# Row tiles turned by a product with identity times root, and first products made tile by tile, in an encoder step

## The chip, the cores and the metric

The kernel runs on one core of one Trainium2 chip. The metric is device time in microseconds, the median of repeated runs. The kernel before the change takes 1940.13 us (three runs, 1940.03 to 1941.39). One execution of it was profiled: 1939.99 us, with a span of 1938.3 us from its first profiled instruction to its last.

## The reference, cut to what matters

One layer of a streaming encoder is computed for 1024 new frames of a prompt and 32 frames of a running stream, 1056 tokens of width 2048 in all:

```
h = rms_norm(x, norm_pre)            # x * rsqrt(mean(x*x) + 1e-6) * gain
p = h @ w_in                         # 2048 x 6656, split into three groups of heads
o = concat(stick-breaking attention, sliding window, chunk band), each times silu(gate)
y = x + rms_norm(o @ w_out, norm_post)
```

All inputs are float32. The change touches `rms_norm(x, norm_pre)`, the transposition of its result, and the first of the 128-column tiles of `h @ w_in`.

## The kernel before, in words

TensorE contracts over partitions, so `h` has to lie with its 2048 features on partitions: `act_hi` and `act_lo`, each 128 x 16 x 1056 (feature within a block, block, token). `act_hi` is the value rounded to the reduced float32 type (fp32r), `act_lo` is what the rounding left. A weight piece is split in the same way into `w_hi` and `w_lo`, and a product is three fp32r matmuls: `w_hi` with `act_hi`, `w_hi` with `act_lo`, `w_lo` with `act_hi` (lines 1194, 1195, 1196 in `product`). The weights are the operand that stays in the array and are loaded before each matmul (LDWEIGHTS); the activations are the operand that moves through it.

The tokens come in nine row tiles, eight of 128 tokens and one of 32. For each row tile `t`:

- SyncE loads it into one of four buffers `x_t` (line 1031); tile `t + 4` waits until tile `t` has been transposed.
- ScalarE squares it with a sum per row (`x_squares`, line 1490). GpSimd makes the variance of that (line 2128), ScalarE a first guess of the reciprocal root by a logarithm and an exponential (`x_guess`, lines 1496 and 1498), GpSimd refines it with four tiny instructions (lines 2130 to 2136).
- VectorE multiplies the row tile by the root and by the norm weights in one instruction over 2048 columns (`x_scale`, line 1738).
- TensorE transposes the 16 blocks of 128 columns in four groups of four, each group into one PSUM bank (`x_tile`, line 1184). The block is the operand that stays, the identity the one that moves.
- ScalarE copies each bank to `act_hi` (`x_high`, line 1503) and VectorE subtracts that from the bank into `act_lo` (`x_low`, line 1745).

The tokens also form three groups of 352 for the projection, one PSUM bank each. The first weight tile has four pieces (`q` = 0 to 3, four blocks of features each). Its pieces are rounded by ScalarE (`high`, line 1508) and split by VectorE (`low`, line 1753) after row tile 2. `first_project(g, quarters)` runs `product(g, q)`, 12 matmuls of 352 moving columns: group 0 after row tiles 3, 4 and 5, group 1 after row tiles 6, 7 and 8, group 2 after all. Each of these calls follows `x_tile(t)` in TensorE's order, which is the order of the program text. VectorE's order is `x_scale(0)`, then for each `t`: `x_scale(t + 1)`, `x_low(t)`, and after `t` = 2 the four `low`.

After that a plan that is fixed in the program interleaves the other 51 weight tiles with attention (`pe_plan`), and last comes the output projection. SyncE issues the loads of weight pieces in its own planned order; a piece of the second weight tile waits until the last use of the piece before it (`piece_used`, raised by group 2).

Of the kernel before, what the change touches and what calls it, by code (L numbers as in the profile page):

```python
# [10 lines left out]
P = 128  # L11
# [529 lines left out]
def build(nc, x_prompt, x_sample, cache_a_k, cache_a_v, cache_b_k, cache_b_v, cache_c_k, cache_c_v,  # L541
# [3 lines left out]
    with ctx:  # L545
# [12 lines left out]
        def sem(name):  # L558
            return ctx.enter_context(nc.semaphore(name))
# [43 lines left out]
        x_t = [arena[:, o:o + D] for o in (1152, 1152 + D, 1152 + 2 * D, 1152 + 4 * D + D // 2)]  # L603
        pre_gain = arena[:, 1152 + 3 * D:1152 + 4 * D]
        squares_x = arena[:, 1152 + 4 * D:1152 + 4 * D + D // 2].bitcast(BF16)

# [93 lines left out]
        def bank(b, n=512, r=P, c=0):  # L700
            return ps[0:r, 512 * b + c:512 * b + c + n]
# [49 lines left out]
        x_in = [sem(f"x_in{i}") for i in range(4)]  # L751
        gain_in = sem("gain_in")
        x_sq, x_var, x_ln, x_std, x_rstd, x_norm = (sem(n) for n in ("x_sq", "x_var", "x_ln", "x_std", "x_rstd", "x_norm"))
# [420 lines left out]
        def _(pe):  # L1174
            mm = nc.tensor.matmul

            def x_tile(t):
                rows = rows_of(t)
                for g in range(4):
                    pe.wait_ge(x_norm, t + 1)  # L1180
                    if t:
                        pe.wait_ge(x_lo, 4 * t + g - 3)
                    for c in range(4):
                        last = nc.tensor.transpose(bank(X + g, rows, P, rows * c),
                                                   x_t[t % 4][0:rows, P * (4 * g + c):P * (4 * g + c) + P],
                                                   ident[0:rows, 0:rows])
                    last.then_inc(xt_done, 1)
# [22 lines left out]

            def first_project(g, *quarters):
                pe.wait_ge(x_lo, 4 * (3 * g + 3))
                for q in quarters:
                    pe.wait_ge(lo_made, q + 1)
                    last = product(g, q)
                    if q == 3:
                        last.then_inc(proj_done, 1)
                    elif g == GROUPS - 1:
                        last.then_inc(piece_used, 1)

            def set_ready(key):
# [202 lines left out]
            for t in range(TT + 1):  # L1424
                x_tile(t)

                if t >= 3:
                    first_project(t // 3 - 1, *((0,), (1, 2), (3,))[t % 3])
            first_project(GROUPS - 1, 0, 1, 2, 3)

# [51 lines left out]
        def _(act):  # L1482
# [9 lines left out]
            def x_guess(t):  # L1492
                rows = rows_of(t)
                r = std_x[0:rows, t % 3:t % 3 + 1]
                act.wait_ge(x_var, t + 1)
                fn(r, var[0:rows, t:t + 1], ACT.Ln).then_inc(x_ln, 1)
                act.wait_ge(x_ln, t + 1)
                fn(r, r, ACT.Exp, scale=-0.5).then_inc(x_std, 1)
# [7 lines left out]
            def high(T, q):  # L1506
                act.wait_ge(raw_in[q], RAW[T])
                fn(w_hi[:, q, :], w_raw[:, q, :], ACT.Copy).then_inc(hi_made, 1)  # L1508
# [4 lines left out]
            for t in range(TT + 1):  # L1513

                if t < TT - 1:
                    x_squares(t + 2)
                x_high(t, 0)
                x_high(t, 1)
                if t < TT - 1:
                    x_guess(t + 2)  # L1520
                x_high(t, 2)
                x_high(t, 3)
                if t == 2:
                    for q in range(4):
                        high(0, q)

# [196 lines left out]
        def _(dve):  # L1723
            v = nc.vector

            v.memset(qbd[:, :], 0.0).then_inc(zeroed, 1)

            dve.wait_ge(rel_in, 16)
# [4 lines left out]

            def x_scale(t):
                rows = rows_of(t)
                r = std_x[0:rows, t % 3:t % 3 + 1]
                dve.wait_ge(x_rstd, 4 * t + 4)
                v.scalar_tensor_tensor(x_t[t % 4][0:rows, :], x_t[t % 4][0:rows, :], r, pre_gain[0:rows, :],  # L1738
                                       ALU.mult, ALU.mult).then_inc(x_norm, 1)

# [13 lines left out]

            x_scale(0)
            for t in range(TT + 1):
                if t < TT:
                    x_scale(t + 1)
                x_low(t)
                if t == 2:  # L1760
                    for q in range(4):
                        low(q)

# [340 lines left out]
        def _(pool):  # L2104
# [7 lines left out]
            for m in (ident, ident_b):  # L2112
# [8 lines left out]
                             pattern=[[1, DEC]], channel_multiplier=-1).then_inc(consts, 1)  # L2121

            for t in range(TT + 1):

# [3 lines left out]
                gp.tensor_scalar(var_, ssq[0:rows, t:t + 1], 1.0 / D, EPS, ALU.mult, ALU.add).then_inc(x_var, 1)  # L2128
                pool.wait_ge(x_std, t + 1)
                gp.tensor_tensor(nt, r, r, ALU.mult).then_inc(x_rstd, 1)  # L2130
                pool.wait_ge(x_rstd, 4 * t + 1)
# [3 lines left out]
                pool.wait_ge(x_rstd, 4 * t + 3)  # L2135
                gp.tensor_tensor(r, r, nt, ALU.mult).then_inc(x_rstd, 1)

            gp.memset(mask_c[:, :], 0.0).then_inc(consts, 1)
# [103 lines left out]
```

## Time and profile before

| | |
|---|---|
| median of three runs | 1940.13 us |
| profiled execution | 1939.99 us |
| its span | 1938.3 us |
| TensorE busy in the span | 1907.4 us (98%) |
| VectorE busy | 1221.8 us (63%) |
| ScalarE busy | 667.4 us (34%) |
| GpSimd busy | 51.9 us (3%) |

A profile page names engines PE (TensorE matmul), PEld (TensorE weight load, which overlaps PE), DVE (VectorE), ACT (ScalarE), POOL (GpSimd) and SP (SyncE). Times are microseconds from the start of the span, unless marked ns. Matmuls are pipelined: the duration of one holds its way through the array, and the distance from the start of one to the start of the next is what it costs in a stream. Some matmul records are missing from a trace, so counts of long stretches run a few per cent low.

### The profile page before, as it was taken

The numbers are of one execution on the slowest core, as the hardware profiler recorded it, in microseconds if no ns is written. First come the engines' busy times: TensorE is split into PE (matmuls) and PEld (weight loads), VectorE is DVE, ScalarE is ACT, GpSimd is POOL, SyncE is SP. The second block draws the span as 40 slices with busy tenths as digits, with TensorE's granted clock in tenths as the row PEclk, the third lists the DMA queues.
The fourth block names the chain that finished last, engine by engine and source line by source line (L and its number), as shares of the span: only waits on it lengthen the run. The fifth ranks groups of instructions, "written<-read, shape, count | busy, mean of one in ns | idle before, by whom it ended". The sixth has DMA issues, their size and how long they took to land.

```text
span 1938.3 us, 31051 instructions
## 1 busy us (share of the span) xinstructions
PE 1907.4 (98%) x12604; PEld 1751.8 (90%) x12604; DVE 1221.8 (63%) x2176; ACT 667.4 (34%) x1257; POOL 51.9 (3%) x119
## 2 busy tenths in 40 slices
PE   5999999999999999999999999999999999999997
PEld 5999999999999999999999999999999988888886
DVE  7358677786877778554544454355525666766878
ACT  7124333343423334221222222233213354344453
POOL 3000000000000000000000000000000000000131
PEclk9999999999999999999999999999999999999999
DMA  6446777676777766666657657465446557555396
GB/s 245 117 115 140 156 154 166 144 147 153 151 156 155 170 139 144 157 136 134 154 117 154 147 129 143 104 145 123 107 97 145 131 195 284 192 175 187 122 257 226
DMA packets 880406, 301.05 MB, mean 155 GB/s; under 512 B 618504, under 2 KB 845592, under 8 KB 878968
## 3 DMA queue, kind: packets, MB, share of 16 engines
q1 hardware_dynamic: 877192, 290.35, 61.6%
q0 software_dynamic: 3072, 8.73, 2.2%
q8 instruction: 99, 1.62, 0.3%
q14 instruction: 43, 0.35, 0.1%
HBM read 210.45 MB, written 96.20 MB: 158 GB/s over the span
## 4 chain that ended last, share of the span: by engine, by line
PE 94%; DVE 4%; DMA 1%; issue 1%; ACT 0%; POOL 0%; DVEq 0%; SPq 0%; ACTq 0%; POOLq 0%
PE ps L1194 23%; PE ps L1195 22%; PE ps L1196 22%; PE ps L1405 4%; PE ps L1407 4%; PE ps L1406 4%; PE ps L1297 3%; PE ps L1376 3%; PE ps L1258 3%; PE ps L1347 3%; DVE arena L1738 1%; DVE act_lo L1745 1%; PE ps L1402 1%; PE ps L1401 1%; DMA arena<-in_x_prompt_dram 0%
## 5 line engine op out<-in xcount | busy, mean ns | idle before, releaser
L1194 PE MATMUL ps<-act_hi,w_hi 128*128 128x352 f32 x2688 | 877.8, 327 | 0.0
L1195 PE MATMUL ps<-act_lo,w_hi 128*128 128x352 f32 x2688 | 862.7, 321 | 0.0
L1196 PE MATMUL ps<-act_hi,w_lo 128*128 128x352 f32 x2688 | 862.6, 321 | 0.0
L1194 PEld LDWEIGHTS ps<-act_hi,w_hi 128*128 128x128 f32 x2688 | 504.6, 188 | 16.9 <-issue 14.0
L1195 PEld LDWEIGHTS ps<-act_lo,w_hi 128*128 128x128 f32 x2688 | 505.5, 188 | 0.0
L1196 PEld LDWEIGHTS ps<-act_hi,w_lo 128*128 128x128 f32 x2688 | 504.3, 188 | 0.0
L1508 ACT ACTIVATE w_hi<-w_raw 128x512 fp32r<-128x512 f32 x224 | 139.2, 623 | 344.7 <-DMA w_raw<-in_w_in_dram 344.6
L1753 DVE TENSOR_TENSOR w_lo<-w_raw,w_hi 128x512 fp32r<-128x512 f32 x224 | 150.5, 673 | 51.9 <-ACT w_hi L1508 51.7
L1575 ACT ACTIVATE arena<-arena,small 128x257 f32<-128x257 f32 (+6 forms) x180 | 101.2, 565 | 208.2 <-DVE small L1886 208.2
L2074 DVE STREAM_TRANSPOSE arena<-arena 128x1024 f32<-128x1024 f32 (+4 forms) x100 | 132.6, 1326 | 49.4 <-ACT arena L1696 48.6
L1696 ACT ACTIVATE arena<-arena 128x1024 f32<-128x1024 f32 (+1 forms) x60 | 61.1, 1018 | 251.8 <-DVE arena L1860 251.8
L1405 PE MATMUL ps<-w_hi,l_hi 128*128 128x512 f32 x280 | 109.3, 390 | 0.6 <-DVE w_lo L1944 0.3
L1407 PE MATMUL ps<-w_hi,l_lo 128*128 128x512 f32 x280 | 109.0, 389 | 0.0
L1406 PE MATMUL ps<-w_lo,l_hi 128*128 128x512 f32 x280 | 108.9, 389 | 0.0
L1886 DVE CUSTOM_DVE_ANT_0 arena<-ps,arena 128x640 f32<-128x640 f32 (+5 forms) x72 | 44.0, 660 | 85.7 <-PE ps L1297 85.7
L1836 DVE TENSOR_TENSOR arena<-ps,arena 128x1024 f32<-128x1024 f32 (+1 forms) x60 | 70.2, 1171 | 30.9 <-ACT arena L1692 30.9
L1777 DVE COPY arena<-ps 128x352 f32<-128x352 f32 x84 | 43.1, 515 | 64.9 <-PE ps L1196 63.3
L1848 DVE TENSOR_TENSOR_SCAN arena<-arena 128x512 f32<-128x512 f32 (+4 forms) x102 | 79.5, 833 | 0.8
L1692 ACT ACTIVATE arena<-arena 128x1024 f32<-128x1024 f32 (+1 forms) x60 | 61.1, 1019 | 52.2 <-DVE arena L2084 52.2
L1587 ACT ACTIVATE w_hi<-w_raw 128x512 fp32r<-128x512 f32 x70 | 44.0, 628 | 101.2 <-DVE w_raw L1923 79.0
L1688 ACT ACTIVATE arena<-ps 128x1024 f32<-128x1024 f32 (+1 forms) x60 | 58.6, 976 | 55.0 <-PE ps L1275 47.1
L1786 DVE TENSOR_SCALAR arena<-ps 128x352 f32<-128x352 f32 x48 | 25.1, 523 | 76.9 <-PE ps L1196 76.7
(183 smaller groups left out, 2097.3 us busy)
## 6 DMA issues: line engine op xcount, KB each, us to landing
w_raw<-in_w_in_dram SPq DMA_DIRECT2D x176, 256.0 KB, 3.3
weight_scratch<-arena SPq DMA_DIRECT2D x216, 128.0 KB, 3.5
arena<-weight_scratch SPq DMA_DIRECT2D x54, 512.0 KB, 4.6
b_out<-in_w_out_dram SPq DMA_DIRECT2D x72, 256.0 KB, 3.3
w_raw<-in_w_out_dram SPq DMA_DIRECT2D x70, 256.0 KB, 2.6
w_raw<-in_w_in_dram SPq DMA_DIRECT2D x96, 128.0 KB, 3.1
weight_scratch<-arena SPq DMA_DIRECT2D x80, 132.0 KB, 4.0
arena<-weight_scratch SPq DMA_DIRECT2D x40, 256.0 KB, 3.4
```

Of the source, the lines that this page charges most:

```text
L1194: mm(bank(g, GN), wh, ah, start=(k == 0), stop=False)
L1195: mm(bank(g, GN), wh, al, start=False, stop=False)
L1196: last = mm(bank(g, GN), wl, ah, start=False, stop=(k == KT - 1))
L1405: mm(out, th, wh, start=first, stop=False)
L1406: mm(out, th, wl, start=False, stop=False)
L1407: last = mm(out, tl, wh, start=False, stop=end)
L1508: fn(w_hi[:, q, :], w_raw[:, q, :], ACT.Copy).then_inc(hi_made, 1)
L1575: fn(s, s, ACT.Exp, bias=neg_max[0:rows_of(m), t:t + 1], scale=-1.0, accum_out=row_sum[0:rows_of(m), t:t + 1]).then_inc(p_exp, 1)
L1753: v.tensor_tensor(w_lo[:, slot, :], w_raw[:, slot, :], w_hi[:, slot, :].bitcast(F32), ALU.subtract).then_inc(lo_made, 1)
L1836: v.tensor_tensor(both, z, both, ALU.max).then_inc(sp_ready, 1)
L1848: v.tensor_tensor_scan(along, along, along, 0.0 if newest else carry[:, 2 * m - 8 + h:2 * m - 7 + h], ALU.add, ALU.max).then_inc(sum_ready, 1)
L2074: v.transpose(s, s).then_inc(wt_blocks, 1)
```

## The change

VectorE no longer multiplies by the root. It multiplies each row tile by the norm weights alone (`x_gain`, a tensor_tensor over 2048 columns), which no longer waits for the root: only for the row tile and for its squares (tiles 1 and 2 write to other places and don't wait for their squares). GpSimd makes a diagonal matrix for each tile, identity times root (`scale_d`), and TensorE turns each block by a plain float32 matmul with that matrix as the moving operand, where it had a transpose with the identity. GpSimd also rounds the four first weight pieces, which ScalarE did. The first guess of the root reads the sums of squares directly. The first weight tile's products are no longer made per group of 352 tokens but in column ranges a..b of groups 0 and 1, as the row tiles arrive; group 2 stays whole.

```diff
             def x_tile(t):
                 rows = rows_of(t)
                 for g in range(4):
                     pe.wait_ge(x_norm, t + 1)
+                    pe.wait_ge(diag_made, t + 1)
                     if t:
                         pe.wait_ge(x_lo, 4 * t + g - 3)
                     for c in range(4):
-                        last = nc.tensor.transpose(bank(X + g, rows, P, rows * c),
-                                                   x_t[t % 4][0:rows, P * (4 * g + c):P * (4 * g + c) + P],
-                                                   ident[0:rows, 0:rows])
+                        last = mm(bank(X + g, rows, P, rows * c), x_gained(t, rows)[:, 4 * g + c, :],
+                                  scale_d[t % 3][0:rows, 0:rows], start=True, stop=True)
...
+            def first_product(g, q, a, b):
+                for kk in range(4):
+                    k = 4 * q + kk
+                    wh, wl = w_hi[:, q, P * kk:P * kk + P], w_lo[:, q, P * kk:P * kk + P]
+                    ah, al = act_hi[:, k, GN * g + a:GN * g + b], act_lo[:, k, GN * g + a:GN * g + b]
+                    out = bank(g, b - a, P, a)
+                    mm(out, wh, ah, start=(k == 0 and a == 0), stop=False, skip_group_check=True)
+                    mm(out, wh, al, start=False, stop=False, skip_group_check=True)
+                    last = mm(out, wl, ah, start=False, stop=(k == KT - 1), skip_group_check=True)
+                return last
...
+            EARLY = {1: [(0, 0, P, 0, 1)], 2: [(0, 0, P, 2, 3), (0, P, 2 * P, 0, 1, 2, 3)], 3: [(0, 2 * P, GN, 0, 1, 2, 3)],
+                     4: [(1, 0, 4 * P - GN, 0, 1)], 5: [(1, 0, 4 * P - GN, 2, 3)],
+                     6: [(1, 4 * P - GN, GN, 0, 1)], 7: [(1, 4 * P - GN, GN, 2, 3)]}
...
-                if t >= 3:
-                    first_project(t // 3 - 1, *((0,), (1, 2), (3,))[t % 3])
-            first_project(GROUPS - 1, 0, 1, 2, 3)
+                for part in EARLY.get(t, ()):
+                    first_project(*part)
+            first_project(GROUPS - 1, 0, GN, 0, 1, 2, 3)
...
             def x_guess(t):
...
-                act.wait_ge(x_var, t + 1)
-                fn(r, var[0:rows, t:t + 1], ACT.Ln).then_inc(x_ln, 1)
+                act.wait_ge(x_sq, t + 1)
+                act.wait_ge(eps_made, 1)
+                fn(r, ssq[0:rows, t:t + 1], ACT.Ln, bias=eps_col[0:rows, :], scale=1.0 / D).then_inc(x_ln, 1)
...
+                for g in range(4):
+                    x_high(t, g)
                 if t < TT - 1:
                     x_squares(t + 2)
-                x_high(t, 0)
-                x_high(t, 1)
-                if t < TT - 1:
                     x_guess(t + 2)
-                x_high(t, 2)
-                x_high(t, 3)
-                if t == 2:
-                    for q in range(4):
-                        high(0, q)
...
-            def x_scale(t):
+            def x_gain(t):
                 rows = rows_of(t)
-                r = std_x[0:rows, t % 3:t % 3 + 1]
-                dve.wait_ge(x_rstd, 4 * t + 4)
-                v.scalar_tensor_tensor(x_t[t % 4][0:rows, :], x_t[t % 4][0:rows, :], r, pre_gain[0:rows, :],
-                                       ALU.mult, ALU.mult).then_inc(x_norm, 1)
+                dve.wait_ge(x_in[t % 4], 16 * (t // 4 + 1))
+                if t not in (1, 2):
+                    dve.wait_ge(x_sq, t + 1)
+                v.tensor_tensor(x_gained(t, rows), x_t[t % 4].rearrange("p (k c) -> p k c", c=P)[0:rows],
+                                pre_gain.rearrange("p (k c) -> p k c", c=P)[0:rows], ALU.mult).then_inc(x_norm, 1)
...
+                if t == 1:
+                    low(0)
+                    low(1)
                 x_low(t)
-                if t == 2:
-                    for q in range(4):
-                        low(q)
+                if t == 1:
+                    low(2)
+                    low(3)
...
+            def first_high(q):
+                pool.wait_ge(raw_in[q], RAW[0])
+                gp.tensor_copy(w_hi[:, q, :], w_raw[:, q, :]).then_inc(hi_made, 1)
...
+                pool.wait_ge(x_rstd, 4 * t + 4)
+                if t >= 3:
+                    pool.wait_ge(xt_done, 4 * (t - 3) + 4)
+                gp.tensor_scalar(scale_d[t % 3][0:rows, 0:rows], ident[0:rows, 0:rows], r, None, ALU.mult).then_inc(diag_made, 1)
+                if t in (1, 2):
+                    first_high(2 * t - 2)
+                    first_high(2 * t - 1)
```

`first_project(g, a, b, quarters)` waits for the row tiles that hold the tokens up to `b` of group `g` and runs `first_product(g, q, a, b)` for each quarter.

## Rows read from the trace of the kernel before

**Rows 1.** The page: shares of the span, and the chain that ended last.

```profile
PE 1907.4 (98%) x12604; PEld 1751.8 (90%) x12604; DVE 1221.8 (63%) x2176; ACT 667.4 (34%) x1257; POOL 51.9 (3%) x119
...
PE 94%; DVE 4%; DMA 1%; issue 1%; ACT 0%; POOL 0%; DVEq 0%; SPq 0%; ACTq 0%; POOLq 0%
```

**Rows 2.** Busy time by stretch: start:end, length, engines, granted clock, DMA.

```profile
12.15:50.00 37.85, 30.54 (x186) 27.31 (x187) 35.40 (x40) 34.06 (x67) 16.31 (x43) 0.95 0.60 205
57.30:65.00 7.70, 7.70 (x51) 7.70 (x50) 1.15 (x3) 1.26 (x2) 0.00 (x0) 1.00 0.30 84
65.00:1700.00 1635.00, 1635.00 (x11321) 1523.05 (x11321) 1000.29 (x1830) 515.46 (x952) 0.00 (x0) 1.00 0.65 147
```

**Rows 3.** Chain that ended last, in order of time: start, length, what.

```profile
14.60 2.35 DVE arena L1738
16.95 2.39 DVE act_lo L1745 x4
...
48.03 2.42 PE ps L1184 x16
```

**Rows 4.** Timeline of TensorE's matmuls: start, length, what, count.

```profile
12.15 3.65 PE L1184 MATMUL ps<-ident,arena 128*128 128x128 f32 x16 [12.15 <-DVE arena L1738]
17.70 3.31 PE L1184 MATMUL ps<-ident,arena 128*128 128x128 f32 x16 [1.90 <-DVE act_lo L1745]
...
54.21 1.19 PE L1184 MATMUL ps<-ident,arena 32*128 32x32 f32 x16
55.32 0.43 PE L1194 MATMUL ps<-act_hi,w_hi 128*128 128x352 f32 x1
...
55.91 0.32 PE L1194 MATMUL ps<-act_hi,w_hi 128*128 128x352 f32 x1
...
57.34 0.32 PE L1194 MATMUL ps<-act_hi,w_hi 128*128 128x352 f32 x1
...
223.66 2.00 PE L1258 MATMUL ps<-arena 64*128 64x512 f32 x12
225.59 0.51 PE L1275 MATMUL ps<-mask_b,ident_b 128*128 128x128 bf16 x6
```

**Rows 5.** Groups of matmuls by line and shape: count, busy, mean ns.

```profile
L1258 PE MATMUL ps<-arena 64*128 64x512 f32 x144 | 37.4, 624 | 0.0
```

**Rows 6.** Line 1258 alone in two short stretches: how many matmuls had begun.

```profile
223.60:223.65 0.05, 0.00 (x0) 0.00 (x0) 1.00 1.12 338
223.65:223.70 0.05, 0.04 (x2) 0.04 (x2) 1.00 1.10 328
```

**Rows 7.** Timeline of TensorE's weight loads: start, length, what, count.

```profile
54.20 1.08 PEld L1184 LDWEIGHTS ps<-ident,arena 32*128 32x128 f32 x16 [0.21 <-issue]
55.32 0.19 PEld L1194 LDWEIGHTS ps<-act_hi,w_hi 128*128 128x128 f32 x1
55.43 0.19 PEld L1195 LDWEIGHTS ps<-act_lo,w_hi 128*128 128x128 f32 x1
55.59 0.19 PEld L1196 LDWEIGHTS ps<-act_hi,w_lo 128*128 128x128 f32 x1
```

**Rows 8.** Timeline of ScalarE, VectorE and GpSimd.

```profile
7.51 0.19 ACT L1490 ACTIVATION_READ_ACCUMULATOR arena<-arena 128x1 f32 x1
...
8.24 0.20 ACT L1498 ACTIVATE small<-small 128x1 f32<-128x1 f32 x1
...
10.72 1.91 ACT L1490 ACTIVATE arena<-arena 128x2048 bf16<-128x2048 f32 x1 [2.27 <-DMA arena<-in_x_prompt_dram]
...
9.65 2.35 DVE L1738 SCALAR_TENSOR_TENSOR arena<-arena,small 128x2048 f32<-128x2048 f32 x1 [2.40 <-POOL small L2136]
...
54.98 1.05 DVE L1745 TENSOR_TENSOR act_lo<-ps,act_hi 128x128 fp32r<-128x128 f32 x4 [0.66 <-ACT act_hi L1503]
...
8.52 0.19 POOL L2130 TENSOR_TENSOR small<-small 128x1 f32<-128x1 f32 x1 [0.55 <-ACT small L1498]
8.79 0.19 POOL L2132 TENSOR_TENSOR small<-small 128x1 f32<-128x1 f32 x1
...
15.45 1.55 POOL L2128 TENSOR_SCALAR small<-small 128x1 f32<-128x1 f32 x1 [0.89 <-ACT arena L1490]
```

**Rows 9.** VectorE's split of the first weight pieces, and GpSimd's nearest 128x128 operation.

```profile
28.57 2.49 DVE L1753 TENSOR_TENSOR w_lo<-w_raw,w_hi 128x512 fp32r<-128x512 f32 x4
...
2.87 0.29 POOL L2113 TENSOR_SCALAR_AFFINE_SELECT ident<-ident 128x128 f32<-128x128 f32 x1 [0.24 <-POOL mask_s L2110]
```

More of the change, by code:

```diff
@@ L604, in build, with x_gained @@
         pre_gain = arena[:, 1152 + 3 * D:1152 + 4 * D]
+        eps_col = small[:, 149:150]
+        x_early = place("x_early", [P, KT, TOK], F32, 0, 0)
+        scale_d = [arena[:, 12416 + P * i:12416 + P * i + P] for i in range(3)]
+        def x_gained(t, rows):
+            if t == 1:
+                return raw[:, :, SEQ - P:SEQ]
+            if t == 2:
+                return x_early[:, :, SEQ - P:SEQ]
+            return x_t[t % 4].rearrange("p (k c) -> p k c", c=P)[0:rows]
         squares_x = arena[:, 1152 + 4 * D:1152 + 4 * D + D // 2].bitcast(BF16)
@@ L751, in build @@
         x_in = [sem(f"x_in{i}") for i in range(4)]
-        gain_in = sem("gain_in")
+        gain_in, eps_made, diag_made = sem("gain_in"), sem("eps_made"), sem("diag_made")
         x_sq, x_var, x_ln, x_std, x_rstd, x_norm = (sem(n) for n in ("x_sq", "x_var", "x_ln", "x_std", "x_rstd", "x_norm"))
@@ L1209, in project, with first_project @@
                     last.then_inc(piece_used, 1)
-            def first_project(g, *quarters):
-                pe.wait_ge(x_lo, 4 * (3 * g + 3))
+            def first_product(g, q, a, b):
[8 more added lines that the diff above has]
+                return last
+            def first_project(g, a, b, *quarters):
+                end = GN * g + b
+                pe.wait_ge(x_lo, 4 * min((end - 1) // P + 1, TT + 1))
                 for q in quarters:
                     pe.wait_ge(lo_made, q + 1)
-                    last = product(g, q)
-                    if q == 3:
+                    last = first_product(g, q, a, b)
+                    if q == 3 and b == GN:
                         last.then_inc(proj_done, 1)
-                    elif g == GROUPS - 1:
+                    elif q < 3 and g == GROUPS - 1:
                         last.then_inc(piece_used, 1)
+            EARLY = {1: [(0, 0, P, 0, 1)], 2: [(0, 0, P, 2, 3), (0, P, 2 * P, 0, 1, 2, 3)], 3: [(0, 2 * P, GN, 0, 1, 2, 3)],
+                     4: [(1, 0, 4 * P - GN, 0, 1)], 5: [(1, 0, 4 * P - GN, 2, 3)],
+                     6: [(1, 4 * P - GN, GN, 0, 1)], 7: [(1, 4 * P - GN, GN, 2, 3)]}
             def set_ready(key):
@@ L1726, in _ @@
             v.memset(qbd[:, :], 0.0).then_inc(zeroed, 1)
+            v.memset(eps_col, EPS).then_inc(eps_made, 1)
             dve.wait_ge(rel_in, 16)
@@ L1753, in low @@
                 v.tensor_tensor(w_lo[:, slot, :], w_raw[:, slot, :], w_hi[:, slot, :].bitcast(F32), ALU.subtract).then_inc(lo_made, 1)
-            x_scale(0)
+            x_gain(0)
             for t in range(TT + 1):
                 if t < TT:
-                    x_scale(t + 1)
+                    x_gain(t + 1)
+                if t == 1:
+                    low(0)
+                    low(1)
                 x_low(t)
-                if t == 2:
-                    for q in range(4):
-                        low(q)
+                if t == 1:
+                    low(2)
+                    low(3)
             def tile_out(T, g):
@@ L2121, in _ @@
                              pattern=[[1, DEC]], channel_multiplier=-1).then_inc(consts, 1)
+            pool.wait_ge(consts, CONSTS)
+            def first_high(q):
+                pool.wait_ge(raw_in[q], RAW[0])
+                gp.tensor_copy(w_hi[:, q, :], w_raw[:, q, :]).then_inc(hi_made, 1)
             for t in range(TT + 1):
@@ L2129, in _ @@
                 pool.wait_ge(x_std, t + 1)
+                pool.wait_ge(x_var, t + 1)
                 gp.tensor_tensor(nt, r, r, ALU.mult).then_inc(x_rstd, 1)
```

## The prediction

> **What bounds the kernel now.** I read the page first. TensorE is busy 98% of the span and holds 94% of the chain that ended last, VectorE 4% [rows 1]. Then busy time by stretch: from 65 to 1700 us TensorE has no gap at all; the only idle time before it lies ahead of 57.3 us, and from 12.15 to 50 us it is busy 30.54 of 37.85 us, in part at a lowered clock [rows 2]. So what matters of a change to the first tiles is one moment: when TensorE ends the first weight tile. Whatever that moment moves by, the end of the kernel moves by. The chain in order of time shows who sets it now: VectorE alternates the scaling (2.35 us) and four subtractions (2.39 us) up to 48.03 us, where TensorE takes over with the transposes of tile 7 [rows 3]. From there TensorE runs without a wait: the products' matmuls are 0.159 us apart (nine steps from 55.91 to 57.34), group 1's last quarter begins at 55.32 and has 12 of them [rows 4], so group 2 with its 48 starts at about 57.3 and ends at 57.3 + 7.6 = **64.95 us**. TensorE began at 12.15 us [rows 4]: 52.8 us for the first weight tile.
>
> The 52.8 us hold 8 x 2.42 [rows 3] + 1.1 [rows 4] of transposes and 144 x 0.159 = 22.9 of products, 43.4 in all. Idle time and half clock are thus **9.4 us**. That is all there is to win, and the work that the change adds to TensorE has to fit in it.
>
> **The change part by part.**
>
> *The turn by a product.* A transpose of a 128x128 float32 block is one matmul. In tile 7, 16 take 2.42 us [rows 3]: four groups of 0.60, which is 4 x 0.109 and 0.165 for the waits at the group's head. What does a plain float32 matmul cost? The nearest is line 1258, the scores (64 rows, 128 weights). The program asks for 72 of 512 columns there (six units, six pieces, two heads); the trace has 144 [rows 5]: each plain float32 matmul is two instructions. Twelve of them (4 x 512, 4 x 384, 4 x 128 columns, 4096 in sum) take 225.59 - 223.66 = 1.93 us [rows 4]. Two begin within the same 0.05 us [rows 6]: the two heads lie in different halves of the array and run side by side, so the stream is 2048 columns in 1.93 us, 0.94 ns a column, 0.12 us for 128 with the change of mode; the transposes' 0.109 is the same rate without that. So one block costs 2 x 0.109 = 0.218 us where it cost 0.109. Per tile: 32 x 0.109 + 4 x 0.165 = **4.14 us instead of 2.42**. For the seven tiles 1 to 7 this adds 12.0 us, for tile 0 another 1.7. Bounds: 2.42 (one instruction will do, as for the transpose) and, with loading not hidden behind moving, 0.22 each, 7.6 us.
>
> The tile of 32 rows: 16 instructions took 1.1 us, their weight loads 0.068 apart [rows 4, 7]. Now there are 32, with plain loads of 128 columns at 0.109: 3.5 us, bounds 2.2 (at 0.068) and 3.9.
>
> *The narrow products.* Groups 0 and 1 are cut in ranges of 128, 128, 96 and of 160, 192 columns. The number of matmuls goes from 96 to 144 + 96 = 240. With 352 columns, loading the next weights hides behind the 0.159 us of moving. Where nothing holds a load back, the next begins 0.11 us later (55.32 to 55.43); after that they keep the matmuls' pace [rows 7]. With 192 columns or fewer the moving takes less than that (0.159 x 192/352 = 0.087), so the loads set the pace: **240 x 0.110 = 26.4 us instead of 96 x 0.159 = 15.3**, 11.1 more. Bounds: below, the loads go at the 0.068 of the 32-row transposes, and a matmul costs the greater of that and its columns: 144 x 0.068 + 48 x 0.072 + 48 x 0.087 = 17.4; above, a narrow fp32r matmul is as slow as plain float32, four times the rate of columns: 48 x (0.218 + 0.218 + 0.164 + 0.27 + 0.33) = 57.6. I take 0.110, the nearest row: same line, same type, same load.
>
> The Trainium skill, "TensorE: Matmul & The Clock Gate", section "Back-to-back issue gap", gives about 81 ns for a pair of load and matmul with 128 columns in a real kernel, and its section on loading gives columns/1.2, 107 ns for 128. The two speak for different sums: by the first, an estimate from that page, the 240 matmuls take some 20 us and the forecast falls by 6; by the second, nothing changes. The row at 55.43 sides with the second.
>
> *Waits in front of the products.* There are 20 quarters before group 2, where there were 8. Most waits are long satisfied; none shows at 55.32, while a group's head in the transposes costs 0.165. I take 0.1 us for 12 more, 1.2 us; between 0 and 2.0.
>
> *VectorE.* The gain alone is a tensor_tensor of 2048 columns. Four of 512 from the same kinds of operand take 2.49 us [rows 9], the old instruction 2.35 [rows 8]: I cost it at 2.35 (bounds 2.3 and 2.5), no gain: nine of them, hidden behind TensorE from here on. Its waits get shorter: tile 0 from 9.65 to 7.8, after the sum of squares is read at 7.70; tile 1 from 14.60 to 10.75, when its data is there [rows 3, 8].
>
> *GpSimd and the root of tile 0.* The guess no longer waits for GpSimd and ends at about 8.25. The four refinements and the diagonal (0.29, nearest: an operation of that size [rows 9]) take 4 x 0.275 + 0.3 = 1.4 us. But GpSimd stands still while VectorE runs on two operands in SBUF: its instruction at 15.45 took 1.55 us instead of 0.19 and ended at 17.00, when VectorE's scaling (14.60 to 16.95) ended [rows 3, 8]. Before, the scaling waited for GpSimd, so the root of tile 0 was never in its way; now the gain of tile 0 runs from 7.8 to 10.15 just as the root is due, and the gain of tile 1 from 10.75 to 13.1. Two of the five instructions fit in between; the rest follows at 13.1: diagonal at 13.9, first matmul at **14.0 instead of 12.15**, 1.85 later. Bounds: no blocking, 10.3 (after the gain of tile 0); all five after 13.1, 14.7. The Trainium skill, "SBUF — State Buffer", section "SBUF: two separate sides", says that the pair of ports is locked for a whole VectorE instruction with two SBUF inputs, which takes in the new tensor_tensor; no run here shows that form against GpSimd.
>
> *Rounding by GpSimd, ScalarE's order, loads.* ScalarE has per tile four copies, a square and two guesses, some 4.5 us, against TensorE's 6.8 or more: hidden. The load of tile 4 waits for tile 0's turn and comes later (19.2 for 15.8); TensorE comes to that tile at about 48. The second weight tile's pieces wait for group 2, as before, and move with it. Cost 0. VectorE's sum is about 44 us from 7.8, it is no longer the pace.
>
> **The sum.** TensorE starts at 14.0. Tile 0 at half clock first: before, the clock had not risen at 17.70 and 16 transposes took 3.31 us [rows 4]; a transpose every 0.21 us, 1.2 GHz, where tile 7 had one every 0.109 at 2.4. I count 16 instructions at 0.213 and 16 at 0.109, 5.2 us: 19.2. Tile 1, 4.1: 23.3. The first range needs `low(0)`: tile 0's last subtraction ends at 20.8, gain of tile 2 until 23.1, `low(0)` until 23.7: 0.4 idle. Then without a break: tiles 2 to 7 6 x 4.14 = 24.8; tile 8 3.5; products 26.4; group 2 7.6; waits 1.2: 63.5. End at 23.7 + 63.5 = **87.2 us**, 22.3 after 64.95. Everything behind moves with it: the profiled execution of 1939.99 becomes **1962.3 us**; it lies 0.14 below the median, which I leave out.
>
> **The rivals.**
>
> 1. *Loads are faster than 0.110 in a stream of narrow matmuls* (0.068 to 0.09), or GpSimd is not blocked. For it: the 32-row transposes. Against it: two starts 0.11 apart on the very lines. 5 to 9 us less for the products, 1.3 in tile 8, up to 3.7 for the start: 1948 to 1957.
> 2. *Narrow fp32r matmuls run at the rate of plain float32.* No row has fewer than 352 columns. 57.6 - 26.4 = 31 more: 1993.
> 3. *TensorE is priced by moving columns alone, and only once for the turn.* For it: a transpose and this matmul move the same 128 columns, and total columns of the products don't change. Then nothing is added to TensorE, VectorE stays the pace and its chain of subtractions starts at about 16.6 instead of 16.95 [rows 3] with all the work it had. Its last subtraction, which ended at 56.03 [rows 8], ends at 55.7, and group 2 can follow at once: 63.3, 1.6 earlier, 1938.4; and with GpSimd not blocked 5 us earlier, 1935. It decides where the added work is under 9.4 - 1.85 = 7.5 us; I count 29.5. Against it: the 144 instructions for 72 matmuls, and the 0.11.
>
> Even rival 3 gains little, since VectorE's work per tile stays 4.7 us.
>
> **How the numbers follow.** Forecast 0.68; rival 1 0.17; rival 2 0.07; rival 3 0.05, of which two thirds are within 0.2%; something else slower 0.03. Below 0.2% (3.9 us) a measurement of this kernel can hardly tell a change from none. The forecast's own range is 1957 to 1970 (tiles at 4.14 to 4.5, half clock for 3 to 7 us, start 12 to 14.7). The range over cases 1 and the forecast is 1948 to 1973. Faster 0.02, within 0.2% 0.04, slower 0.94.
>
> **What would show it.** Right: line `x_tile` has 32 matmuls of 128x128 per tile, some 4.1 us; the narrow products start 0.11 us apart; VectorE waits for TensorE and not the reverse from 26 us on; the first `x_tile` starts at about 14, with GpSimd's root instructions stretched to the end of a gain; the first product of the second weight tile starts near 87 us, and the rest of the trace is the old one moved by 22. Wrong: 16 instructions a tile, narrow products at 0.07 or at 0.2, idle time of TensorE between 26 and 87 us, or a gain given back behind 87.

## The result and the profile after

The changed kernel takes 1964.8 us (median of four runs, 1962.29 to 1966.96) where the kernel before takes 1940.76: the ratio is 1.012, 95% interval 1.0108 to 1.0133. It is slower by 24 us. A second set of runs (below) gives 1.0125, 1.011 to 1.014. The profiled execution took 1962.29 us, 22.3 more than the 1939.99 of the one before; its span is 1960.5 us, 22.2 more than 1938.3. It is the fastest of its four runs.

First the page of the changed kernel, the lines that answer to [rows 1]:

```profile
PE 1933.6 (99%) x12892; PEld 1781.0 (91%) x12892; DVE 1223.6 (62%) x2177; ACT 668.7 (34%) x1253; POOL 67.5 (3%) x132
...
PE 95%; DVE 2%; issue 1%; DMA 1%; POOL 0%; ACT 0%; DVEq 0%; SPq 0%; ACTq 0%; POOLq 0%
```

TensorE is busy 26 us longer, and VectorE's share of the chain has halved. In the first tiles TensorE waited for VectorE before; now VectorE waits for TensorE. Busy time by stretch shows where (start:end, length, engines, granted clock, DMA), beside [rows 2]:

```profile
14.32:24.00 9.68, 8.95 (x66) 8.79 (x66) 5.88 (x7) 6.17 (x12) 4.36 (x11) 1.00 0.80 244
24.00:77.00 53.00, 52.50 (x464) 52.26 (x463) 34.03 (x41) 30.31 (x54) 24.97 (x49) 0.98 0.37 126
77.00:87.20 10.20, 10.01 (x48) 10.01 (x49) 1.60 (x6) 1.26 (x2) 0.00 (x0) 0.75 0.23 68
87.20:1700.00 1612.80, 1612.80 (x11223) 1504.63 (x11222) 981.36 (x1800) 507.05 (x938) 0.00 (x0) 1.00 0.65 146
```

From 24 us on TensorE is full up to 1700 us but for 0.69 us before group 2; VectorE works 34 of 53 us where it had worked 35.4 of 37.85 [rows 2]. The granted clock of the first stretch reads 1.00, but the pace of the instructions says otherwise: up to about 17.2 us they are 0.21 us apart, which is the pace of 1.2 GHz, and then 0.11. TensorE's timeline, against [rows 4]:

```profile
14.32 5.20 PE L1197 MATMUL ps<-arena 128*128 128x128 f32 x32 [14.32 <-POOL arena L2175]
19.36 3.74 PE L1197 MATMUL ps<-arena,raw 128*128 128x128 f32 x32
23.83 0.30 PE L1229 MATMUL ps<-act_hi,w_hi 128*128 128x128 f32 x1 [0.73 <-DVE w_lo L1778]
...
24.86 0.28 PE L1229 MATMUL ps<-act_hi,w_hi 128*128 128x128 f32 x1
24.97 0.28 PE L1230 MATMUL ps<-act_lo,w_hi 128*128 128x128 f32 x1
25.08 0.28 PE L1231 MATMUL ps<-act_hi,w_lo 128*128 128x128 f32 x1
...
26.53 3.79 PE L1197 MATMUL ps<-arena,x_early 128*128 128x128 f32 x32
30.07 0.31 PE L1229 MATMUL ps<-act_hi,w_hi 128*128 128x128 f32 x1
...
45.05 0.28 PE L1229 MATMUL ps<-act_hi,w_hi 128*128 128x96 f32 x1
45.16 0.27 PE L1230 MATMUL ps<-act_lo,w_hi 128*128 128x96 f32 x1
...
64.97 0.27 PE L1230 MATMUL ps<-act_lo,w_hi 128*128 128x192 f32 x1
65.08 0.28 PE L1231 MATMUL ps<-act_hi,w_lo 128*128 128x192 f32 x1
...
72.21 4.29 PE L1197 MATMUL ps<-arena 32*128 32x32 f32 x32
...
77.19 0.66 PE L1229 MATMUL ps<-act_hi,w_hi 128*128 128x352 f32 x1 [0.69 <-DVE act_lo L1770]
77.65 0.49 PE L1230 MATMUL ps<-act_lo,w_hi 128*128 128x352 f32 x1
```

The turn of a tile is 32 matmuls, 3.54 us from 26.53 to 30.07 (before, 2.42 for the 16 transposes of tile 7 [rows 3]). Products of 128 columns start 0.112 us apart (24.86, 24.97, 25.08), and so do those of 96, 160 and 192. Group 2 begins at 77.19, and from its second matmul on they are 0.29 apart (77.65, 77.94), where 352 columns take 0.16. Busy time by stretch, cut where the pace changes, shows what happened:

```profile
72.21:75.25 3.04, 3.04 (x29) 3.04 (x28) 0.58 (x2) 0.69 (x3) 0.64 (x2) 1.00 1.15 370
75.25:82.10 6.85, 6.16 (x24) 6.02 (x24) 0.86 (x4) 0.41 (x2) 0.00 (x0) 0.50 0.41 144
```

The granted clock fell to 0.50, which is 1.2 GHz, in the middle of the tile of 32 rows. TensorE had not been idle since 23.83 us; its next idle time, the 0.69 us before group 2, came only behind the fall.

The timelines of VectorE and of GpSimd show the start of all that, beside [rows 8]; the gains of VectorE run from 8.38 to 10.67 and from 10.85 to 13.14:

```profile
8.38 2.29 DVE L1763 TENSOR_TENSOR arena<-arena 128x2048 f32<-128x2048 f32 x1 [0.66 <-DMA arena<-in_norm_pre_dram]
10.85 2.29 DVE L1763 TENSOR_TENSOR raw<-arena 128x2048 f32<-128x2048 f32 x1 [0.18 <-DMA arena<-in_x_prompt_dram]
```

```profile
8.52 2.20 POOL L2165 TENSOR_TENSOR small<-small 128x1 f32<-128x1 f32 x1 [0.28 <-ACT small L1527]
10.80 0.19 POOL L2167 TENSOR_TENSOR small<-small 128x1 f32<-128x1 f32 x1
11.07 2.12 POOL L2169 TENSOR_SCALAR small<-small 128x1 f32<-128x1 f32 x1
13.27 0.19 POOL L2171 TENSOR_TENSOR small<-small 128x1 f32<-128x1 f32 x1
13.56 0.61 POOL L2175 TENSOR_SCALAR arena<-ident,small 128x128 f32<-128x128 f32 x1
```

Two instructions on 128x1 elements last 2.20 and 2.12 us, each until a gain has ended.

The plan behind the first tiles has a landmark, its first scores. In TensorE's timeline of the two kernels, before and after:

```profile
112.78 1.13 PE L1258 MATMUL ps<-arena 64*128 64x512 f32 x4
```

```profile
135.14 1.13 PE L1286 MATMUL ps<-arena 64*128 64x512 f32 x4
```

They begin 22.4 us later, and the span is 22.2 us longer. Within 0.2 us nothing is lost or won behind.

### The profile page after: what moved, and what is told of

The parts are those of the page before. It is cut to its first block, busy times and chain, and to the rows that moved or that the text cites. A ratio compares the mean times of both kernels' runs of the same rounds, so it can differ in the third digit from the quotient of the medians.

```text
span 1960.5 us, 31673 instructions
## 1 busy us (share of the span) xinstructions
PE 1933.6 (99%) x12892; PEld 1781.0 (91%) x12892; DVE 1223.6 (62%) x2177; ACT 668.7 (34%) x1253; POOL 67.5 (3%) x132
## 3 DMA queue, kind: packets, MB, share of 16 engines
q8 instruction: 102, 1.67, 0.3%
## 4 chain that ended last, share of the span: by engine, by line
PE 95%; DVE 2%; issue 1%; DMA 1%; POOL 0%; ACT 0%; DVEq 0%; SPq 0%; ACTq 0%; POOLq 0%
PE ps L1206 22%; PE ps L1207 21%; PE ps L1208 21%; PE ps L1433 4%; PE ps L1435 4%; PE ps L1434 4%; PE ps L1325 3%; PE ps L1404 3%; PE ps L1286 3%; PE ps L1375 3%; PE ps L1197 2%; PE ps L1430 1%; PE ps L1429 1%; PE ps L1229 1%; PE ps L1231 1%
## 5 line engine op out<-in xcount | busy, mean ns | idle before, releaser
L1206 PE MATMUL ps<-act_hi,w_hi 128*128 128x352 f32 x2640 | 861.7, 326 | 0.0
L1208 PE MATMUL ps<-act_hi,w_lo 128*128 128x352 f32 x2640 | 847.4, 321 | 0.0
L1207 PE MATMUL ps<-act_lo,w_hi 128*128 128x352 f32 x2640 | 847.3, 321 | 0.0
L1206 PEld LDWEIGHTS ps<-act_hi,w_hi 128*128 128x128 f32 x2640 | 495.5, 188 | 16.9 <-issue 14.0
L1207 PEld LDWEIGHTS ps<-act_lo,w_hi 128*128 128x128 f32 x2640 | 496.4, 188 | 0.0
L1208 PEld LDWEIGHTS ps<-act_hi,w_lo 128*128 128x128 f32 x2640 | 495.2, 188 | 0.0
```

Of the source, the lines that this page charges most:

```text
L1206: mm(bank(g, GN), wh, ah, start=(k == 0), stop=False)
L1207: mm(bank(g, GN), wh, al, start=False, stop=False)
L1208: last = mm(bank(g, GN), wl, ah, start=False, stop=(k == KT - 1))
```

## Experiments

Times are medians, of four runs where no number is given; "ratio" is against the kernel before on the same chip, with its 95% interval. Of each variant one execution was profiled, so what its trace shows can differ from what its median shows.

### The changed kernel again

> The changed kernel once more, to see what its own times spread over. In its profile TensorE's granted clock fell to 1.2 GHz at 75.3 us, in the middle of the tile of 32 rows, and came back at 82.1, though TensorE had not stopped; its four times lay in two pairs, 1962.3 to 1963.2 and 1966.4 to 1967.0. Theory: the pairs differ in how long the clock stays low here: 1962 to 1967 again, and a profile near 1966 shows the low clock some 7 us longer or a second time. Rival: the times vary for another reason, somewhere else in the kernel.

1965.66 us, ratio 1.0125 (1.011 to 1.014), four runs from 1964.63 to 1967.17. The profiled execution (1964.63) has the same low clock in the same place, and its first scores even begin at 134.78 us, 0.4 earlier. Its 2.3 us over the other profile arise behind that. So the theory of the pairs isn't borne out by this profile: between executions some 2 us move in the planned part too. There TensorE is idle for 0.56 us between 400 and 800 us, where the other profile has no idle time.

### The tile of 32 rows with 128 moving columns

```diff
-                        last = mm(bank(X + g, rows, P, rows * c), x_gained(t, rows)[:, 4 * g + c, :],
-                                  scale_d[t % 3][0:rows, 0:rows], start=True, stop=True)
+                        last = mm(bank(X + g, P, P, P * c), x_gained(t, rows)[:, 4 * g + c, :],
+                                  scale_d[t % 3][0:rows, :], start=True, stop=True)
...
```

GpSimd makes the diagonal of this tile 128 columns wide, and ScalarE and VectorE read the first 32 of each 128 columns from PSUM; these edits are left out above.

> The matmuls of the tile of 32 rows move 128 columns of the diagonal instead of 32 (the other 96 are zeros that nobody reads). Their weight loads are the same, 0.11 us apart, so their pace should not change. Theory: the clock falls because in these 32 matmuls the array is fed for a quarter of the time only; with 128 columns it stays at 2.4 GHz, TensorE ends the first weight tile at about 83.8 us instead of 87.2, and the time is 1959, without the spread of 4 us. Rival (the clock falls for another reason, such as few rows in use): 1962 to 1967 as before the edit. Rival (wider matmuls cost their columns): 1 to 3 us slower.

1965.86 us, ratio 1.0123 (1.0108 to 1.0138). No gain. The matmuls cost no more for their columns (32 in 3.83 us, all at the high clock), but the clock fell right behind them, and once more in an earlier place. Busy time by stretch, the changed kernel first:

```profile
40.00:60.00 20.00, 20.00 (x182) 20.00 (x181) 12.80 (x15) 13.53 (x22) 6.55 (x13) 1.00 0.31 102
60.00:90.00 30.00, 29.31 (x209) 29.07 (x208) 14.22 (x23) 10.36 (x20) 8.71 (x18) 0.89 0.38 121
```

```profile
40.00:60.00 20.00, 20.00 (x153) 20.00 (x152) 9.89 (x10) 10.32 (x18) 4.88 (x8) 0.83 0.21 68
60.00:90.00 30.00, 29.31 (x228) 29.02 (x227) 14.92 (x23) 13.17 (x25) 10.69 (x24) 0.94 0.39 126
```

With the two levels 1.00 and 0.50, a mean clock c over a stretch of length L means 2 x (1 - c) x L at 1.2 GHz: here 6.8 us in the first stretch, during and behind the products of 96 columns, and 3.6 in the second, against 0 and 6.6 in the changed kernel. Its first scores begin at 138.37. That a quarter of the columns moved is what makes the clock fall in this tile is not borne out: the variant of the gain of tile 1 (below), whose last tile moves 32 columns as before, has the same two low stretches (0.83 and 0.94).

### The last tile taken apart

```diff
-            for t in range(TT + 1):
+            for t in range(TT - 1):
                 x_tile(t)
...
+            x_tile(TT - 1)
+            first_project(1, 4 * P - GN, GN, 2)
+            x_tile(TT, (0, 1))
+            first_project(1, 4 * P - GN, GN, 3)
+            x_tile(TT, (2, 3))
```

The second argument of `x_tile` names the groups that are turned.

> The changed kernel with the four groups of the tile of 32 rows taken apart: two between the last two quarters of group 1 (192 columns each), two behind them. Nothing is added or left out. In four profiles TensorE's clock fell during or right after that tile. Theory (32 matmuls of 32 columns in a row make the clock fall): taken apart it stays up, group 2 ends 3.4 us earlier, about 1962. Rival (narrow matmuls of any kind around it are enough): the clock falls all the same, 1965.

1969.5 us, ratio 1.014 (1.0125 to 1.0155), four runs from 1964.24 to 1970.52: the slowest of all, with the same work. Busy time by stretch and the first scores:

```profile
40.00:60.00 20.00, 20.00 (x153) 20.00 (x152) 9.79 (x10) 10.22 (x18) 4.79 (x8) 0.83 0.21 69
60.00:90.00 30.00, 29.31 (x210) 28.86 (x209) 13.88 (x21) 12.38 (x23) 10.54 (x24) 0.83 0.36 116
```

```profile
141.56 1.13 PE L1286 MATMUL ps<-arena 64*128 64x512 f32 x4
```

TensorE was not idle for a moment in the first stretch and for 0.69 us in the second, and had the low clock for 6.8 + 10.2 = 17.0 us. Against the changed kernel that is 10.4 us more, of which half is lost: 5.2; another 1.4 is lost because the clock rose later, in tile 0 (at about 20.2 us instead of 17.2). Sum 6.6, and the first scores come 6.4 us later. The accounting closes. The rival stands: taking the tile apart does not keep the clock up. How much the edit itself made worse is open: the order of the work differs only from the last tiles on, behind 70 us, so of the 10.4 us only what is in the second stretch can come from it.

### The gain of tile 1 after the diagonal of tile 0

```diff
             def x_gain(t):
                 rows = rows_of(t)
+                if t == 1:
+                    dve.wait_ge(diag_made, 1)
```

> VectorE's gain of tile 1 waits until GpSimd has made the diagonal of tile 0. Theory (GpSimd stands still while VectorE has two operands in SBUF): the last two refinements and the diagonal follow the gain of tile 0 at 10.7 us without the 2.1 us stall, TensorE starts at 12.3 instead of 14.3, and the time falls by 2 us. The gain of tile 1 then runs from 12.3 to 14.6, before TensorE needs it. Rival (GpSimd is slow there for another reason, such as waits of its own): the same start, no change or up to 2 us slower.

1964.09 us, ratio 1.0113 (1.0098 to 1.0128). GpSimd's timeline:

```profile
8.28 2.32 POOL L2167 TENSOR_TENSOR small<-small 128x1 f32<-128x1 f32 x1 [0.18 <-ACT small L1527]
10.67 0.19 POOL L2169 TENSOR_TENSOR small<-small 128x1 f32<-128x1 f32 x1
10.95 0.19 POOL L2171 TENSOR_SCALAR small<-small 128x1 f32<-128x1 f32 x1
11.23 0.19 POOL L2173 TENSOR_TENSOR small<-small 128x1 f32<-128x1 f32 x1
11.52 0.61 POOL L2177 TENSOR_SCALAR arena<-ident,small 128x128 f32<-128x128 f32 x1
```

The second stall is gone, the third refinement lasts 0.19 us, and TensorE starts at 12.28 instead of 14.32. So the stall came from the gain that was moved. Less than the 2.0 us arrive: by the medians 1.6, hardly clear of the spread, and in the trace tile 1 begins at 18.64, 0.7 before the changed kernel's, since tile 0 took 6.4 us instead of 5.0. TensorE's clock rose no sooner: the pace doubled at about 18 us, where it had at 17.2.

### The first 256 tokens in one range

```diff
-EARLY = {1: [(0, 0, P, 0, 1)], 2: [(0, 0, P, 2, 3), (0, P, 2 * P, 0, 1, 2, 3)], 3: ...
+EARLY = {2: [(0, 0, 2 * P, 0, 1, 2, 3)], 3: ...
```

> The first 256 tokens of group 0 in one range, after row tile 2, instead of twice 128: 48 matmuls of 256 columns in place of 96 of 128. Theory (a matmul costs the greater of 0.112 for its load and its columns): 48 x about 0.12 instead of 96 x 0.112, 5 us less for TensorE; 1 us of that is lost because it has nothing to do after row tile 1. 4 us faster than the changed kernel, about 1959 to 1961. Rival (the cost goes with columns): no less work and less to do early, 1 to 3 us slower.

1961.1 us, ratio 1.0103 (1.0086 to 1.0119): 4.6 us faster than the changed kernel beside it. TensorE's timeline in the new range:

```profile
29.52 0.28 PE L1229 MATMUL ps<-act_hi,w_hi 128*128 128x256 f32 x1
29.64 0.28 PE L1230 MATMUL ps<-act_lo,w_hi 128*128 128x256 f32 x1
29.76 0.27 PE L1231 MATMUL ps<-act_hi,w_lo 128*128 128x256 f32 x1
```

256 columns cost 0.12 us a matmul (48 in 5.74 us), 128 columns 0.112. At the rate of the 352-column products, 0.159 us, 256 columns take 0.116 and 128 columns 0.058: at 256 the columns have caught up with the load, and below that halving the columns saves next to nothing. TensorE waited 2.60 us for the diagonal of tile 2, where 1 was expected, since it has no products to make in between.

### Both edits that took time off

```diff
+EARLY = {2: [(0, 0, 2 * P, 0, 1, 2, 3)], 3: ...
...
+                if t == 1:
+                    dve.wait_ge(diag_made, 1)
```

> The changed kernel with the two edits that took time off it: the gain of tile 1 waits for the diagonal of tile 0, and the first 256 tokens of group 0 are one range. Theory (separate causes that add): 4.5 us from the range and about 1.5 from the start, 1959 to 1960. Rival (the earlier start is lost where TensorE waits for VectorE's split of the first weights and where the clock is still low): 1961, the range alone. Either way slower than the kernel before, since 32 matmuls a tile remain.

1958.84 us, ratio 1.0092 (1.0075 to 1.0109). The two add: 6.8 us off 1965.66, slightly more than was expected. In the traces it is less: the first scores begin at 130.61 us, 1.0 before those with the range alone and 4.5 before the changed kernel's. The turn of 32 matmuls a tile is still there.

### The narrow products alone

The kernel before, with `EARLY`, `first_product` and GpSimd's rounding of the change; `x_scale`, the root and the transposes are untouched.

```diff
-                if t >= 3:
-                    first_project(t // 3 - 1, *((0,), (1, 2), (3,))[t % 3])
-            first_project(GROUPS - 1, 0, 1, 2, 3)
+                for part in EARLY.get(t, ()):
+                    first_project(*part)
+            first_project(GROUPS - 1, 0, GN, 0, 1, 2, 3)
...
+                if t in (1, 2):
+                    first_high(2 * t - 2)
+                    first_high(2 * t - 1)
```

> The kernel before with the narrow products alone: column ranges as in the change, first weights rounded by GpSimd, their split after row tile 1; scaling and transposes as before. Theory (240 loads at 0.112 instead of 96 matmuls at 0.159, less what fills TensorE's idle time): TensorE ends the first weight tile at about 73 instead of 65 us, 1948. Rival (narrow matmuls cost their columns only): the products fill idle time for nothing, 1938 to 1940.

1954.11 us, ratio 1.0065 (1.0051 to 1.0079): 13.3 us slower, where 8 were expected. At the high clock the pace is as expected, 0.112 us, but look at the first of them in TensorE's timeline:

```profile
24.24 0.44 PE L1217 MATMUL ps<-act_hi,w_hi 128*128 128x128 f32 x1 [1.80 <-DVE w_lo L1766]
24.48 0.41 PE L1218 MATMUL ps<-act_lo,w_hi 128*128 128x128 f32 x1
24.70 0.41 PE L1219 MATMUL ps<-act_hi,w_lo 128*128 128x128 f32 x1
```

From the second on they are 0.21 to 0.22 apart: at the low clock the load takes twice as long too. With transposes and idle time in between, that pace lasted until 34.4 us. At the low pace were 24 products (2.5 us lost), the transposes of tile 2 (3.28 us for 1.69) and 8 products more (0.8 us), some 5 us of the 13.3. A second low stretch from 48 to 51.5 us, during and behind the products of 96 columns, cost 1.8, about as much as the one that the kernel before has at 27 us.

### The turn alone

The changed kernel with `first_project(g, quarters)` of before.

```diff
-                for part in EARLY.get(t, ()):
-                    first_project(*part)
-            first_project(GROUPS - 1, 0, GN, 0, 1, 2, 3)
+                if t >= 3:
+                    first_project(t // 3 - 1, *((0,), (1, 2), (3,))[t % 3])
+            first_project(GROUPS - 1, 0, 1, 2, 3)
```

> The changed kernel with the products per group of 352 as before: what is left is the gain without the root, the diagonal by GpSimd, and the turn by a product. Theory: 32 matmuls a tile at 0.112 instead of 16 transposes, and the start 2.2 us later; group 2 ends at 71.5 us, 1947, up to 3 us more if the clock falls at the tile of 32 rows. With the narrow products alone at +8 and this at +7, the two add up to less than the +22 of both, because the 9.4 us of slack can be spent only once. Rival (effects simply add): this one alone is +14, 1954.

1956.06 us, ratio 1.0075 (1.006 to 1.0091): 15.2 us slower, where 7, up to 10 with the clock, were expected. Two things were missing in that. TensorE waited: 2.59 us before tile 2 for GpSimd's diagonal, which the early products of the changed kernel would have filled, and 0.9 more before tiles 3 and 4. And the clock was low for longer: tile 0 took 6.5 us for the 5.04 of the changed kernel, tile 2 5.44, and the mean clock is 0.89 from 24 to 40 and from 60 to 90 us, which is 3.5 and 6.6 us at 1.2 GHz and 5 us lost.

```profile
14.13 6.68 PE L1197 MATMUL ps<-arena 128*128 128x128 f32 x32 [14.13 <-POOL arena L2159]
20.65 3.74 PE L1197 MATMUL ps<-arena,raw 128*128 128x128 f32 x32
26.98 5.44 PE L1197 MATMUL ps<-arena,x_early 128*128 128x128 f32 x32 [2.59 <-POOL arena L2159]
```

13.3 and 15.2 make 28.5, where the whole change costs 24. The parts add to more than the whole, as foreseen: each alone first eats the slack of the kernel before, though each alone also keeps some idle time with a low clock that the whole doesn't have. How much is the one and how much the other these runs don't separate.

### Transposes in place of the product

```diff
-                        last = mm(bank(X + g, rows, P, rows * c), x_gained(t, rows)[:, 4 * g + c, :],
-                                  scale_d[t % 3][0:rows, 0:rows], start=True, stop=True)
+                        last = nc.tensor.transpose(bank(X + g, rows, P, rows * c), x_gained(t, rows)[:, 4 * g + c, :],
+                                                   ident[0:rows, 0:rows])
```

> The changed kernel with a transpose by the identity in place of the product with the diagonal; the root of the first norm is left out of the result, all waits stay. Theory (the product is two instructions where the transpose is one): 16 instead of 32 per tile, some 1.2 to 1.8 us less in each of eight tiles and 2.5 in the last, where the clock stays up; about 1947 to 1949. Rival (the cost lies in the narrow products or the start, not in the turn): within 4 us of the changed kernel.

1954.92 us, ratio 1.0063 (1.0048 to 1.0078); three runs from 1954.3 to 1955.6 and one of 1947.7. TensorE's timeline has 16 per tile again:

```profile
45.83 3.66 PE L1197 MATMUL ps<-ident,arena 128*128 128x128 f32 x16
52.64 1.92 PE L1197 MATMUL ps<-ident,arena 128*128 128x128 f32 x16
```

1.92 us a tile at the high clock, half of the product's 3.74, and 3.66 at the low one. That the product costs twice what the transpose does is shown. The clock was low for 17 us between 24 and 90 us (means 0.80 to 40 us, 0.83 to 60, 0.94 to 90), which costs 8 us; the one run of 1947.7 is where the expectation for a clock that stays up had it, but it has no profile.

### The kernel before, with the first weights split by GpSimd

```diff
+            def first_split(q):
+                pool.wait_ge(raw_in[q], RAW[0])
+                gp.tensor_copy(w_hi[:, q, :], w_raw[:, q, :]).then_inc(hi_made, 1)
+                pool.wait_ge(hi_made, q + 1)
+                gp.tensor_tensor(w_lo[:, q, :], w_raw[:, q, :], w_hi[:, q, :].bitcast(F32), ALU.subtract).then_inc(lo_made, 1)
...
+                if t in (2, 3, 4, 5):
+                    first_split(t - 2)
```

This variant leaves out ScalarE's four `high` and VectorE's four `low`.

> The kernel before with one edit: GpSimd rounds and splits the four first weight pieces (one after each of the row tiles 2 to 5), ScalarE and VectorE no longer do. Theory: up to 48 us VectorE is the pace of the kernel before, and its four splits take 2.4 us of it; without them everything behind moves up, 1937.8, 2.3 us faster than before. GpSimd has room between its roots. Rival (GpSimd's subtraction holds the shared ports and VectorE's scaling waits for it, four times 0.6 us or more): no gain, 1940 to 1941.

1942.65 us (eleven runs), ratio 1.0008 (0.9999 to 1.0017): no gain, if anything a loss. Timelines of GpSimd and of VectorE:

```profile
18.48 0.61 POOL L2119 CAST w_hi<-w_raw 128x512 fp32r<-128x512 f32 x1
19.18 1.27 POOL L2121 TENSOR_TENSOR w_lo<-w_raw,w_hi 128x512 fp32r<-128x512 f32 x1
```

```profile
19.24 3.35 DVE L1735 SCALAR_TENSOR_TENSOR arena<-arena,small 128x2048 f32<-128x2048 f32 x1
```

The block works both ways. GpSimd's subtraction runs from 19.18 to 20.45, and VectorE's scaling, which takes 2.35 us alone, takes 3.35. It is so with each of the four pieces. Four times 1.0 us is 1.6 more than the 2.4 us of the four splits, and the first scores begin 1.65 us later than before, at 114.43 for 112.78.

## Why the prediction was right

The forecast was 1962.3 for the profiled execution, and it took 1962.29; the median is 2.5 higher. That the sum fits this well is in part luck: it was 3.6 us too high for the turns of tiles 2 to 7 and 3.9 too low for the last tile, the wait behind it and group 2. By its steps:

- *TensorE's moment decides.* Right: 64.95 was to become 87.2, and the second weight tile begins at 87.24.
- *Start of the turn.* 14.0, measured 14.32. GpSimd stood still during both gains as foreseen; the 0.3 are the diagonal, which took 0.61 us where I had priced it at 0.29. After that tile 0 took 5.04 for 5.2, tile 1 3.7 for 4.1, and the idle time before the first range was 0.73 for 0.4.
- *The turn by a product.* Two instructions a block, 32 a tile: right, and shown against the transposes by an experiment. The size was off. I had 32 x 0.109 + 4 x 0.165 = 4.14; measured is 3.54, 32 x 0.111 and nothing for the heads of groups. Over tiles 2 to 7 that is 3.6 us less. The 0.165 came from tile 7 of the kernel before [rows 3], and I misread it: it is no cost of a group. Each group of tile 7 waits for VectorE's subtraction of the same group of tile 6, and those are 0.60 us apart; "from there TensorE runs without a wait" was wrong for this tile. Tile 5, for which nothing had to be waited, shows it:

```profile
40.15 1.91 PE L1184 MATMUL ps<-ident,arena 128*128 128x128 f32 x16
47.20 2.48 DVE L1745 TENSOR_TENSOR act_lo<-ps,act_hi 128x512 fp32r<-128x512 f32 x4
```

  The next product follows tile 5 at 41.82, so 16 transposes cost 1.67 us (1.74 in tile 6), about half of 3.54. Hence the time that TensorE could have won was not 9.4 but about 15 us: 52.8 - (8 x 1.7 + 1.1 + 22.9) = 15.2. The forecast of the end does not use that number, but rival 3 does.
- *Narrow products.* 0.110, measured 0.112; with 240 of them 26.9 for 26.4. The bounds of 0.068 and of four times the columns are both ruled out. The Trainium skill, "TensorE: Matmul & The Clock Gate", section "Back-to-back issue gap", gives some 81 ns for 128 columns; the fp32r products here take 112, so the forecast would have been worse by it. The same page's section "LDWEIGHTS (loading the stationary operand)" gives columns/1.2, 107 ns for 128, which agrees within 5% at the high clock; at the low clock the trace has 213.
- *Waits.* 1.2, measured 0.3 in front of the narrow products: from 23.83 to 72.21 us they take 27.2 besides the six turns, for 240 x 0.112 = 26.9. The wait that came was one I had at nothing, 0.69 before group 2, for VectorE's last subtraction.
- *What I did not have: a clock that falls again.* Group 2 took 10.05 us for 7.6 and the last tile 4.3 for 3.5. I counted half clock for tile 0 only, since TensorE would be busy nearly without a break from there. It was, and the clock fell nevertheless, for 6.85 us in the changed kernel, at a price of some 3.2: 2.5 in group 2 and 0.7 in the last tile. In the variants it was low for up to 17 us between 24 and 90 us. The median lies 2.5 us above the profiled time, which is that of the fastest run; what it is made of is not shown. The two profiles of this kernel have the same low stretch, and what differs between them, some 2 us, arises in the planned part.
- *Rivals.* 1 and 2 fell by the 0.112. 3, in which columns alone count, fell twice: 32 instructions, and 0.112 for 96 columns as for 192. By the measured prices the change adds 8 x (3.54 - 1.7) = 14.7 us for the turns of 128 rows, 2.5 for the last tile and 26.9 - 15.3 = 11.6 for the products, 28.8 in all, and 2.2 for the later start. From 14.32 to 87.24 are 72.9 us, of which the work takes 66.4; so of the 15.2 us of waiting and low clock 6.5 stayed or came anew, and 8.7 were filled. 28.8 + 2.2 - 8.7 = 22.3.

Open stays what decides whether the clock falls. In the changed kernel and its variants the low stretches between 40 and 90 us begin during the products of 96 columns or during or right behind the last tile (with the tile taken apart, between its halves). Neither moving more columns nor taking the tile apart kept it up. The traces show one thing that goes with it: where the pace of tile 0 doubled by 17.3 us (both profiles of the changed kernel, the range of 256, both edits) only the late stretch came, and where it doubled at about 18 us or later (the wide last tile, the last tile taken apart, the gain of tile 1 alone, the transposes) the clock fell at 43 to 47 us too. Since code that is the same up to there did both, the edits to the last tile are not the reason for the early stretch.

## What to carry to other kernels

Before work is cut smaller so that it can begin earlier, ask for the fixed price of each cut: here a load of 128 columns of float32 or fp32r weights took 0.11 us at the high clock, so a matmul of 96 columns cost what one of 192 did. An early start gains nothing for TensorE if its additional instructions take longer than the idle time that they fill. And a stretch that looks like the cost of the engine can be the pace of another: the 2.42 us of a tile's transposes were VectorE's. Folding a scale into a float32 transpose by a product turns one instruction into two. Moving a small chain to GpSimd, or letting VectorE start early, put the one in the other's way where VectorE had two operands in SBUF.

## What the runs showed of the hardware

- fp32r matmuls with 128 loaded columns start 0.112 us apart for 96, 128, 160 and 192 moving columns, 0.117 to 0.120 for 256, 0.160 for 352; at the low clock 0.21 for 128 and 0.29 for 352.
- Plain float32, 128x128 by 128 columns: two instructions, 0.111 us each. The transpose: one, 0.104 to 0.109 us.
- TensorE's clock fell to 1.2 GHz while its timeline had shown no idle time for 51 us (changed kernel, from 23.83 to the fall at 75.25), in a stream in which the loads set the pace.
- A VectorE tensor_tensor of two SBUF operands held GpSimd up to its end (2.20 us instead of 0.19), and a GpSimd subtraction of 1.27 us held VectorE up by 1.0. The Trainium skill, "SBUF — State Buffer", section "SBUF: two separate sides", says that the pair of ports that the two engines share is locked by whichever starts first, for its whole instruction; these runs agree in both directions.
- GpSimd: 0.61 us to scale 128x128 float32 by a column, 0.61 to round 128x512, 1.27 to subtract 128x512.
